# Two attentions of a decoder trunk: each modulation unit of 2048 columns becomes two halves of 1024, in two successive steps

## What is computed

```python
shift, scale, gate = ada_modulate(c, ada_w[i, 0], ada_b[i, 0])   # silu(c) @ w + b, w is 2048 x 6144
h = rms_norm(x, norm_g[i, 0]) * (1.0 + scale) + shift
...                                                              # mix = attention of h
x = x + gate * mix
```

## Time and profile before

| what | value |
|---|---|
| median of 3 runs | 2068.65 us (2064.25 to 2068.7) |
| the profiled execution's own time | 2059.81 us |
| its span, first to last instruction | 2057.7 us |
| mean granted TensorE clock | 0.971 of 2.4 GHz |
| TensorE / VectorE / ScalarE / GpSimd busy | 92% / 76% / 51% / 10% of the span |
| HBM read | 517.53 MB, 253 GB/s over the span |
| units of modulation in the profile | 192, 2352 ns each |

### The profile page before, as it was taken

How to read it: one execution, slowest core, us unless ns; L and a number is a source line. 1 busy time by engine, 2 the same in 40 slices (tenths; PEclk the granted TensorE clock), 3 DMA queues, 4 the chain that set the end, 5 groups by cost and what they waited for, 6 DMA issues and landing times.

```text
span 2057.7 us, 34052 instructions
## 1 busy us (share of the span) xinstructions
PE 1900.3 (92%) x11444; PEld 1636.0 (80%) x11444; DVE 1558.4 (76%) x2447; ACT 1055.6 (51%) x2257; POOL 212.5 (10%) x317
## 2 busy tenths in 40 slices
PE   3279998889999999999999999989999999999998
PEld 2158854666799999997777878777799999998787
DVE  4988843777778888889788888788677777778554
ACT  1145455655545555556445456565455555556443
POOL 1220000442100000000011000052000000000000
PEclk9679998899999999999999999999999999999999
DMA  8979994567588878886997886868566777765555
GB/s 328 411 264 319 341 319 140 190 225 251 190 285 270 280 265 283 266 284 224 316 339 281 278 289 195 303 225 301 179 234 223 225 237 232 224 202 172 177 189 176
DMA packets 210967, 521.25 MB, mean 253 GB/s; under 512 B 23041, under 2 KB 43010, under 8 KB 186018
## 3 DMA queue, kind: packets, MB, share of 16 engines
q1 hardware_dynamic: 180722, 316.19, 47.3%
q0 software_dynamic: 28032, 201.44, 26.8%
q10 hardware_dynamic: 2096, 2.12, 0.3%
HBM read 517.53 MB, written 2.12 MB: 253 GB/s over the span
## 4 chain that ended last, share of the span: by engine, by line
PE 73%; DVE 13%; DMA 9%; ACT 3%; issue 1%; SPq 0%; DVEq 0%; POOLq 0%; ACTq 0%
PE ps L1025 12%; PE ps L1021 12%; PE ps L1022 11%; PE ps L924 10%; PE ps L920 9%; PE ps L921 9%; DVE acc L1688 6%; DVE ring_lo L1766 3%; DMA ring<-in_od_w_in 2%; DMA ring<-in_ev_w_in 2%; PE ps L759 2%; DMA first_ring<-in_ada_w 1%; DMA aring<-in_ada_w 1%; PE ps L1117 1%; DMA ring<-in_ffn_w_down 1%
## 5 line engine op out<-in xcount | busy, mean ns | idle before, releaser
L1234 ACT ACTIVATE ring_hi<-ring 128x512 fp32r<-128x512 f32 (+2 forms) x1152 | 688.9, 621 | 581.2 <-DMA ring<-in_ffn_w_up 223.4
L1766 DVE TENSOR_TENSOR ring_lo<-ring,ring_hi 128x512 fp32r<-128x512 f32 (+2 forms) x1152 | 742.1, 681 | 283.9 <-ACT ring_hi L1234 282.6
L1021 PE MATMUL ps<-hT_hi,ring_hi 128*128 128x256 f32 x2048 | 512.2, 283 | 1.5 <-issue 0.4
L1022 PE MATMUL ps<-hT_lo,ring_hi 128*128 128x256 f32 x2048 | 507.2, 280 | 0.0
L1022 PEld LDWEIGHTS ps<-hT_lo,ring_hi 128*128 128x128 f32 x2048 | 387.3, 189 | 0.0
L1021 PEld LDWEIGHTS ps<-hT_hi,ring_hi 128*128 128x128 f32 x2048 | 384.7, 188 | 2.3 <-issue 1.2
L1025 PE MATMUL ps<-hT_hi,ring_lo 128*128 128x256 f32 x2048 | 329.2, 282 | 2.4 <-DVE ring_lo L1766 2.4
L1025 PEld LDWEIGHTS ps<-hT_hi,ring_lo 128*128 128x128 f32 x2048 | 279.2, 187 | 2.6 <-DVE ring_lo L1766 2.6
L1688 DVE SCALAR_TENSOR_TENSOR acc<-aring,cs,acc 128x2048 f32<-128x2048 f32 x112 | 263.4, 2352 | 20.1 <-DMA aring<-in_ada_w 8.5
L921 PE MATMUL ps<-ring_hi,hT_lo 128*128 128x512 f32 (+2 forms) x640 | 243.8, 382 | 0.0
L643 POOL DMA_DIRECT2D aring<-in_ada_w x176 | 94.3, 536 | 1379.2 <-DVE acc L1688 1354.8
(11 more groups left out here) (240 smaller groups left out, 2006.7 us busy)
## 6 DMA issues: line engine op xcount, KB each, us to landing
aring<-in_ada_w POOLq DMA_DIRECT2D x176, 1024.0 KB, 6.7
ring<-in_ffn_w_up SPq DMA_DIRECT2D x512, 256.0 KB, 3.0
ring<-in_ffn_w_down SPq DMA_DIRECT2D x256, 256.0 KB, 3.2
ring<-in_od_w_in SPq DMA_DIRECT2D x112, 256.0 KB, 3.6
ring<-in_ev_w_in SPq DMA_DIRECT2D x80, 256.0 KB, 5.6
first_ring<-in_ada_w POOLq DMA_DIRECT2D x16, 1024.0 KB, 6.8
ring<-in_ev_w_out SPq DMA_DIRECT2D x64, 256.0 KB, 3.4
ring<-in_od_w_out SPq DMA_DIRECT2D x64, 256.0 KB, 3.9
```

The lines of the kernel that those rows point to most:

```text
L1021: nc.tensor.matmul(o[q], hi, hT_hi[:, kt, :], start=start, stop=False, skip_group_check=True)
L1022: nc.tensor.matmul(o[q], hi, hT_lo[:, kt, :], start=False, stop=False, skip_group_check=True)
L1234: ins = nc.scalar.activation(out_, in_, f, **kw)
L1766: put(v.tensor_tensor(ring_lo[:, g, part], ring[:, g, part], ring_hi[:, g, part].bitcast(F32), ALU.subtract), lo_ok)
```

## The change

A new helper, `mod_half`, runs the same instruction on 1024 of the 2048 columns. The first half waits for the landing of the unit and raises VectorE's general semaphore; the second half raises `ada_used`. In both attentions, a step that had a unit now has its first half, as the last thing of the step, and the second half is run in the next step, at the same place, in front of the first half of that step's own unit if there is one. After the last step an open second half is run at once. The loads, their order, their waits and the two buffers are untouched, as are the units outside of the attentions.

```diff
+            def mod_half(m, t, col, half):
+
+                slot, landed_, before = mod_slot(m)
+                if half == 0:
+                    dve.wait_ge(landed_, 16 * (before + 1))
+                lane.after()
+                cols = slice(half * 2 * NB, (half + 1) * 2 * NB)
+                put(v.scalar_tensor_tensor(acc[:, t, cols], slot[:, cols], col, acc[:, t, cols], ALU.mult, ALU.add),
+                    ada_used if half == 1 else None)
+
...
+            def rest_half(n, half):
+
+                j = rest_at[n]
+                t, k = MOD_REST[n][j]
+                mod_half(first_mod(n) + len(MOD_PASS[n]) * MOD_PASSES[n] + j, t, cs[:, k:k + 1], half)
+                rest_at[n] += half
...
+                begun = False
                 for n in range(len(units) + LAG + 3):
...
-                    if unit_in_step(n_sub, n):
-                        rest_unit(n_sub)
+                    if begun:
+                        rest_half(n_sub, 1)
+                    begun = unit_in_step(n_sub, n) and rest_at[n_sub] < len(MOD_REST[n_sub])
+                    if begun:
+                        rest_half(n_sub, 0)
+                if begun:
+                    rest_half(n_sub, 1)
```

## The result

| | before | after |
|---|---|---|
| median of 5 runs each | 2068.61 us | 2078.13 us |
| ratio, 95% interval | | 1.0056 [1.0041, 1.0071] |
| profiled execution's own time | 2059.81 us | 2082.43 us |
| its span | 2057.7 us | 2080.3 us |
| mean granted TensorE clock | 0.971 | 0.966 |

The change makes the kernel 11.6 us slower by the ratio (0.0056 x 2068.6; 8.5 to 14.7 by its interval; the medians lie 9.5 us apart). The forecast was 2069.5 us, at about no change; the time lies inside the range, almost on rival 2's 2078.5.

The account below looks back on a forecast made before the run. The prediction took TensorE's waits for VectorE as layer 0's bound, both engines as layer 1's, and the two-buffer ada_w ring at its end. Terms -4.4 and +5.3 gave +0.9 us on 2068.65, so 2069.5 us; range 2059 to 2080.

Parts of the forecast that it names:

- rival 2: Both attentions: loads outlast the time left by buffers held between steps, so stalls lengthen; +9, 2078.5 us; chance 0.22.
- The halves' own cost: Both attentions: a half takes 1284 ns, two take 0.22 us more than one unit, 0.32 with one more gap.
- 1.07 us for each awaited product: Layer 0, steps 1, 3, 11, 19, 27, 35: work ahead of what TensorE awaits shortens; 6.4 us, 5.9 counted.
- Steps 9, 17 and 25: Layer 0: the buffer comes free late, VectorE stands 1.2 us for the load; +0.5 us each, +1.5 together.
- Layer 0 in sum: Layer 0's attention: -5.9 from awaited products and +1.5 from load stalls make -4.4 us, bounds -9 and +2.
- GpSimd's queue: Both attentions: scaling behind the delayed load starts later but stays hidden, with 0.4 to 1.2 us to spare.
- Layer 1: +5.3: Layer 1's attention: load waits end the last unit at 1439.4 to 1441.8, not 1434.68; +5.3 us, bounds +1 and +10.
- The sum: Whole kernel: -4.4 in layer 0 and +5.3 in layer 1 make +0.9 us, so 2069.5 us.
- Rival 1: Lone loads land in 5.1 to 5.2 us and the clock returns; layer 0 gives up to 9; 2061; chance 0.25.
- Rival 3: GpSimd's scaling comes too late in seven cycles of layer 0, ten steps of layer 1; +8.5, 2078; chance 0.08.
- Rival 4: Only the attentions' inner order changes and something else ends each; 2068.6 us; chance 0.05.

Follow-up runs that it names:

- the six places alone: Halves only in steps 1, 3, 11, 19, 27 and 35 of layer 0's attention, all other units whole; against the kernel before: 0.9985 [0.9967, 1.0003].
- the second profile: The changed kernel run and profiled once more, unaltered, against the kernel before: 1.0074 [1.0048, 1.0099].
- the first experiment: Halves in layer 0's attention only, whole units in layer 1's; against the kernel before: 1.0063 [1.0038, 1.0087].
- the scaling first: The changed kernel with GpSimd's scaling of the probabilities queued ahead of the next unit's load; against the kernel before: 1.0067 [1.0042, 1.0091].
- zeros were put in: The changed kernel with six zero products on TensorE ahead of the logits of steps 11, 19 and 27; against the kernel before: 1.0116 [1.0093, 1.0139].
- the two layers alone: Two kernels, halves only in layer 0's or only in layer 1's attention, each against the kernel before: 1.0063 and 1.0042.

## Why the prediction went wrong, point by point

- **The halves' own cost** (1284 ns, +0.22 a pair). Right: 1292 in the mean, 1285 in layer 0, and 2 x 1285 - 2352 = 218 ns more a pair; with the gap between them two halves in a row take 2.68 us, 0.33 more than a whole unit (forecast 0.32). The Trainium skill (Vector Engine (DVE) Microarchitecture Reference, 5.2 Measured stream behaviour on trn2) has some 75 ns for one instruction more in a stream whose instructions overlap. The halves cost more than that; in this kernel each waits for the one before, and no run here lets them overlap.
- **1.07 us for each awaited product.** Right in kind, nearly in size: in the kernel after the waits behind steps 7, 15 and 23 fell from 1.85 to 0.96 us and the cycles without a stall got 1.0 and 0.9 us shorter; with the six places alone those behind steps 11, 19 and 27 fell to 0.7 and 0.8. The six places alone gave -4.5 us in the profile where 5.9 were forecast; steps 1 and 3 of them gave nothing that one profile could show.
- **Steps 9, 17 and 25: +0.5 us each.** This is the step that failed. The order of events was as written: buffer free after the second half, a load issued 0.26 us later, VectorE standing, TensorE waiting "about 3 us" (2.81). But the stall was 2.17 instead of 1.2 us (the landing took 5.85 instead of 5.2, and VectorE asked 0.3 us sooner), and the clock was priced at 0.5 when it took 1.6, 1.8 and 3.1 us. Each cycle cost +2.6, +2.7 and +4.1 instead of +0.5: 9.3 us instead of 1.5. The prediction had the clock's price in its own rows, 1.6 us behind one wait of 1.9 us, and wrote it down as a thing that might come back; behind the longer wait it came once or twice more. The second of its two rows also showed what made this term a gamble: 6.50 us at 1.00 behind a wait of the same length.
- **Layer 0 in sum**: -4.4 forecast, +7.3 in this trace. Up to the first cycle -1.7 (forecast for steps 1, 3 and 7: -3.2), three cycles with a stall +9.3 (forecast +1.5), two without one -1.85 (forecast -2.1), tail +1.6 (forecast -1.07, of step 35). The forecast's parts make -4.4 with the 0.5 left to ScalarE; its +0.5 for a stall's cycle is 1.57 lost at the stall and 1.07 gained behind step 11, 19 or 27. Of the tail's +1.6, some 1.2 are clock in this one execution: in the second profile and in the first experiment the tail took 30.2 us, +0.4. Over the executions with all halves in layer 0 and nothing else changed there (after, after again, layer 0 alone) the attention took 152.4, 153.5 and 146.2 us, and 145.1 and 146.6 with whole units: +4.9 in the mean.
- **GpSimd's queue: hidden.** Wrong in one place: at layer 0's tail TensorE waits 1.34 us for the scaling. There the load stood ahead of the scaling until the second half of a unit was done (issued at 494.07), and the two scalings then took 2.37 us, not 1.8; 0.4 us to spare were not enough. With the scaling first the wait is gone. Beside a whole half, two scalings took 2.2 to 3.0 us in the kernel after, and without one 1.51 at the shortest in layer 0 and 1.84 in layer 1. The Trainium skill (GPSIMD Engine Reference, 8. Key points) says that GpSimd shares its SBUF interfaces with VectorE, with contention when VectorE has two SBUF inputs; the trace agrees by those durations.
- **Layer 1: +5.3.** Right in mechanism, low in size. The first half of step 16's unit was to end at 1416.2; counted from the attention's start it ended at the same place to 0.1 us (1434.20 less the 17.98 us by which this attention started later). From there the loads decided, as said, and the last unit ended at 1441.8 on that scale, the upper end of the 1439.4 to 1441.8. The term that was too small is the landing of step 18's load: 5.8 us in the sum, 7.4 in the trace. It moved the issue of the last load from 1430.2 to 1431.45, and that one landed in 7.7 us. I had taken the lower end on the ground that loads issued further apart land sooner; issued 5.7 to 6.5 us apart, the last four took 7.4 to 8.6. Over all profiles with loads of whole units the attention took 102.4 to 106.3 us with whole units of work (six, mean 103.9) and 110.3 to 113.0 with halves (five, mean 111.3): +7.4.
- **The sum.** 4.9 + 7.4 = 12.3 us from the traces, 11.6 from the runs. I forecast a difference of two terms of about 5; one of them had the wrong sign and the other was some 2 us short.
- **The rivals.** Rival 2 named the mechanism and came to 2078.5, but its +9 had other parts: stalls 2 us longer with the clock at its old price. In the first profile the stalls were 1 us longer and the clock took the rest, so its near hit is in part luck; in the second profile two of three were over 2 us longer, as it said, and the clock came on top. Its point of decision, a load of over 3.8 us, was passed by every load in the earlier trace rows (5.1 at the least), so its chance of 0.22 was too low from the start. The question was never whether the stall comes but what it costs. Rival 1 needed landings of 5.1 to 5.2 us and the clock to come back. In the five profiles with halves of all of layer 0's units and loads of whole ones, the loads of these steps landed in 5.6 to 7.6 us, and no cycle had a higher clock than before except where zeros were put in. Rival 3's mechanism showed once, at the tail; putting the scaling first did not make the kernel faster. Rival 4 is out by the interval.

What stays open: why the same idle time costs clock in one cycle and not in the next, why the same load lands in 5.8 us in one execution and in 7.6 in another, and why the times of the two layers alone add to more than both.

## What to carry to other kernels

Work that is cut in two and spread over two steps holds its buffer from one step into the next: before the instruction, cut the load, or count for each unit the time from the release of its buffer to the next use and compare it with the shortest landing in the trace. Where the time falls short of the landing by even 1 us, price the wait with TensorE's clock behind it and not by its length: read the busy time of the same products in a cycle with such a wait and in one without, in more than one execution. And a gain that is the difference of two terms of the same size is no forecast of "no change", it is two forecasts, each with its own sign.

## What the runs showed of the hardware

A wait of TensorE of 2.6 to 2.9 us, once a cycle of some 20 us, left 80 products at a mean granted clock of 0.91, 0.83 or 0.77 (16.2, 17.7 or 19.15 us busy) without a difference in the wait that I could find, and waits of 4.1 and 4.55 us left them at 0.84 and 0.85 (17.7 us). With TensorE kept busy through it they ran at 1.00 in 14.5 us. The waits of 1.85 us before the change cost some 1.5 us of the same products in the three cycles that hold steps 9, 17 and 25, and nothing in the two between them (14.6 and 14.5 us).

Landing times follow size only in part: 1 MB took 5.1 us at the least and 5.3 in the median in layer 0 of the kernel after, half of it 3.7 and 4.6, an eighth 2.3 and 2.5. Halving a load bought 0.7 to 1.4 us of landing; what it bought beyond that is the earlier release.
